# A hybrid decoder step on one Trainium2 core: keys' rotation partners copied by ScalarE, sigmoids made of Tanh

## The reference, cut to what matters

```python
def partial_rope(x, pos):                       # ROT_DIM = 32 of 128 features, half = 16
    x1, x2 = xf[..., :half], xf[..., half:ROT_DIM]
    out = concatenate([x1 * cos - x2 * sin, x2 * cos + x1 * sin, xf[..., ROT_DIM:]])

aq = partial_rope(rms_norm(aq, q_norm_w), pos)
ak = partial_rope(rms_norm(ak, k_norm_w), pos)

def merge_branches(...):
    h = h * sigmoid(mo)
    h = rms_norm(h, mh_norm_w)
    y_att = (attn * silu(az)) @ w_proj_attn
    y_ml = (h * silu(mz)) @ w_proj_mlstm
    return x + (sigmoid(ga) * y_att + sigmoid(gm) * y_ml) @ w_out
```

## Time and profile before

| what | us |
|---|---|
| median of 3 runs | 475.58 |
| lowest, highest | 474.67, 478.96 |
| the profiled execution | 473.98 |
| its span, first to last instruction | 471.9 |
| TensorE (PE) busy | 459.9 |
| VectorE (DVE) busy | 403.4 |
| ScalarE (ACT) busy | 289.8 |
| GpSimd (POOL) busy | 102.7 |

### The profile page before, as it was taken

How to read it: one execution, slowest core, us unless ns; L and a number is a source line. 1 busy time by engine, 2 the same in 40 slices (tenths; PEclk the granted TensorE clock), 3 DMA queues, 4 the chain that set the end, 5 groups by cost and what they waited for, 6 DMA issues and landing times.

```text
span 471.9 us, 11257 instructions
## 1 busy us (share of the span) xinstructions
PE 459.9 (97%) x3823; PEld 417.8 (89%) x3823; DVE 403.4 (85%) x1646; ACT 289.8 (61%) x486; POOL 102.7 (22%) x181
## 2 busy tenths in 40 slices
PE   7999999999989999999999999999999999999997
PEld 5899899898779899888899879889899898899997
DVE  3898899699999997999999999879999964567861
ACT  4866545676973575895575595658857468334430
POOL 2032321013323322513331242322223110000000
PEclk9999999999999999999999999999999999999999
DMA  8697589747799999999999999999999997456511
GB/s 319 237 386 296 194 316 346 247 179 269 271 417 411 413 394 312 329 405 415 412 397 348 393 411 382 412 398 319 350 413 409 417 413 269 167 181 240 182 75 46
DMA packets 36929, 150.89 MB, mean 320 GB/s; under 512 B 5436, under 2 KB 7036, under 8 KB 29576
## 3 DMA queue, kind: packets, MB, share of 16 engines
q1 hardware_dynamic: 12304, 70.77, 39.4%
q0 software_dynamic: 19008, 67.20, 37.1%
q10 hardware_dynamic: 5560, 12.21, 6.7%
HBM read 137.37 MB, written 12.76 MB: 318 GB/s over the span
## 4 chain that ended last, share of the span: by engine, by line
PE 69%; DVE 13%; ACT 9%; DMA 4%; issue 4%; ACTq 0%; POOL 0%; SPq 0%; DVEq 0%; POOLq 0%
PE pj L533 25%; PE pj L536 12%; PE wk L533 8%; PE pa L714 4%; PE wk L536 4%; DVE w L1070 4%; DVE kpages L1169 3%; DMA cslot<-in_states 2%; ACT w L816 2%; DVE cslot L1253 2%; ACT L836 2%; DMA out_C_s<-cslot 2%; PE wk L486 2%; PE wk L638 1%; PE wk L670 1%
## 5 line engine op out<-in xcount | busy, mean ns | idle before, releaser
L533 PE MATMUL pj<-xn,w 128*128 128x264 f32 x1328 | 180.6, 288 | 0.8 <-ACT mqT L974 0.7
L533 PEld LDWEIGHTS pj<-xn,w 128*128 128x128 f32 x1328 | 168.4, 189 | 8.8 <-issue 6.6
L1070 DVE TENSOR_TENSOR w<-wraw,w 128x1024 fp32r<-128x1024 f32 x112 | 136.1, 1219 | 10.1 <-ACT w L816 9.6
L816 ACT ACTIVATE w<-wraw 128x1024 fp32r<-128x1024 f32 x112 | 117.9, 1053 | 31.6 <-PE wk L536 13.0
L1169 DVE CUSTOM_DVE_ANT_0 kpages<-kpages,qbc 128x128 f32<-128x128 f32 x512 | 114.7, 286 | 0.6 <-DMA kpages<-in_cache_k 0.4
L536 PE MATMUL pj<-xn,w 128*128 128x264 f32 x664 | 94.4, 284 | 3.6 <-DVE w L1070 3.6
L536 PEld LDWEIGHTS pj<-xn,w 128*128 128x128 f32 x664 | 85.5, 188 | 4.7 <-DVE w L1070 4.7
L403 POOL DMA_DIRECT2D kpages<-in_cache_k x64 | 34.3, 536 | 175.5 <-DVE sco L1169 151.8
L403 POOL DMA_DIRECT2D vpages<-in_cache_v x64 | 33.9, 530 | 65.0 <-issue 39.3
L1169 DVE DVE_READ_ACCUMULATOR2_ANT sco<- 128x1 f32 x512 | 40.9, 80 | 0.0
L714 PE MATMUL pa<-vpages,prob 128*32 128x256 f32 x512 | 34.3, 385 | 0.8 <-ACT prob L874 0.8
(11 more groups left out here) (277 smaller groups left out, 640.8 us busy)
## 6 DMA issues: line engine op xcount, KB each, us to landing
wraw<-in_weights SPq DMA_DIRECT2D x56, 1024.0 KB, 7.9
kpages<-in_cache_k POOLq DMA_DIRECT2D x64, 512.0 KB, 8.2
vpages<-in_cache_v POOLq DMA_DIRECT2D x64, 512.0 KB, 10.5
cslot<-in_states SPq DMA_DIRECT2D x16, 512.0 KB, 10.9
out_C_s<-cslot ACTq DMA_DIRECT2D x16, 512.0 KB, 8.0
xres<-in_tokens SPq DMA_DIRECT2D x1, 1056.0 KB, 7.8
out_k_p<-kT ACTq DMA_DIRECT2D x4, 256.0 KB, 11.9
out_v_p<-v_nat ACTq DMA_DIRECT2D x4, 256.0 KB, 6.4
```

The costliest lines, as they stand in the source:

```text
L533: mm(bank[:, 0:T], w2[:, q, 0, k, :], src[:, g, k, :], start=(k == 0 and g == 0), stop=False)
L816: A(w2[:, n % WSPLIT, 0], wraw[:, pair % WRAW, :, (n % 2) * P:(n % 2 + 1) * P], ACT.Copy).then_inc(whi_ready, 1)
L1070: V.tensor_tensor(w2[:, q, 1], wraw[:, slot, :, half * P:(half + 1) * P], w2[:, q, 0], ALU.subtract).then_inc(wlo_ready, 1)
```

## The change

Three things. (1) The features of queries and keys are put in another order by the host, so that a rotated feature's partner stands 32 partitions away (features 0 to 15 in partitions 0 to 15, features 16 to 31 in partitions 32 to 47); constants, norm weights and outputs follow. For the keys, ScalarE copies partitions 32 to 63 of the raw head to partitions 0 to 31 of a new tile `swapped`, and 0 to 31 to 32 to 63; the sign is in the sine table. VectorE reads `swapped` on 64 partitions, and the rotation matmul of the keys is gone, with two waits of TensorE. Queries keep their rotation on TensorE. The decode queries' rows are made by a product with a permutation matrix in place of a transpose. (2) Each sigmoid becomes a Tanh of half the argument; the half and the plus one go into evictions, weights and the products on VectorE. (3) The chain of small gate operations on VectorE, spread over heads 1 to 3, runs at head 0.

```diff
 query_rows (TensorE)
-                    last = tr(bank[0:NB, ...], qT[:, h, SEQ:T], P)
+                    last = mm(bank[0:NB, ...], qT[:, h, SEQ:T], back, start=True, stop=True)
 keys_side (TensorE)
                         pe.wait_ge(c_ready, NB * j - 2) if j else pe.wait_ge(q_ready, HEADS)
-                        pe.wait_ge(attg_ready, 2 * j)
                     else:
                         pe.wait_ge(c_ready, NB * j) if j else pe.wait_ge(qs_ready, 2)
-                        pe.wait_ge(mrs_ready, j + 1)
-                    norm_sums(wk[2 * n], wk[2 * n + 1], n, kT[:, n, :])
+                    mm(wk[2 * n][:, 0:T], ones, sq[:, n, :], start=True, stop=True).then_inc(norm_ps, 1)
 ScalarE
-                A(zsig[:, 1], zraw[:, 1], ACT.Sigmoid).then_inc(sig_ready, 1)
+                A(zsig[:, 1], zraw[:, 1], ACT.Tanh).then_inc(sig_ready, 1)
 (the same at L949, L959 and, with scale=0.5, at L1055; the evictions to zraw get scale 0.5)
-                    A(sq[:, :, :], hT[:, :, :], ACT.Square).then_inc(sqh_ready, 1)
+                    A(sq[:, :, :], hT[:, :, :], ACT.Square, scale=0.5).then_inc(sqh_ready, 1)
                 split_hi(n + AHEAD)
+                if i < 2:
+                    ch.join()
+                    act.wait_ge(kT_ready, 2 * j)
+                    A(swapped[0:LO, i], kT[LO:2 * LO, i, :], ACT.Copy)
+                    A(swapped[LO:2 * LO, i], kT[0:LO, i, :], ACT.Copy).then_inc(swap_ready, 1)
 VectorE
+            ch.step(V.tensor_scalar(mhw, mhw, 0.5, None, ALU.mult))
-            def rope_norm(x, r, ro, done):
-                ch.step(V.tensor_tensor(hT[:, 0, :], ro[:, 0:T], sin, ALU.mult))
-                ch.link(V.tensor_tensor(x, x, cos, ALU.mult))
-                ch.link(V.tensor_tensor(x, x, hT[:, 0, :], ALU.add))
+            def rope_norm(x, r, partners, rows, done):
+                part = slice(0, rows)
+                ch.step(V.tensor_tensor(hT[part, 0, :], partners, sin[part], ALU.mult))
+                ch.link(V.tensor_tensor(x[part], x[part], cos[part], ALU.mult))
+                ch.link(V.tensor_tensor(x[part], x[part], hT[part, 0, :], ALU.add))
                 V.tensor_tensor(x, x, r, ALU.mult).then_inc(done, 1)
-                if h == 1:
+                if h == 0:
                     dve.wait_ge(gate_ln, 1)
...
-                if h == 2:
...
-                if h == 3:
...
-                    dve.wait_ge(norm_ps, HEADS + 2 * j + n + 1)
+                    dve.wait_ge(swap_ready, 2 * j + n + 1)
-                    rope_norm(kT[:, n, :], rs[:, n, :], wk[2 * n + 1], kT_ready)
+                    rope_norm(kT[:, n, :], rs[:, n, :], swapped[:, n, :], 2 * LO, kT_ready)
-                    V.tensor_tensor(zraw[:, 0], zraw[:, 0], zsig[:, 0], ALU.mult).then_inc(silu_ready, 1)
+                    V.scalar_tensor_tensor(out=zraw[:, 0], in0=zsig[:, 0], scalar=1.0, in1=zraw[:, 0], op0=ALU.add, op1=ALU.mult)\
+                        .then_inc(silu_ready, 1)
 (the same form at L1317, L1328, L1418 and L1422; L1432 multiplies by 0.5 as it adds the residual)
```

More of the change, by code:

```diff
@@ L239, in build @@
         rot = cst[:, C_ROT:C_ROT + P]
+        back = cst[:, C_BACK:C_BACK + P]
         mask3 = cst[:, C_MASK:C_MASK + 384]
@@ L561, in query_rows @@
                 for h in range(first, first + 4):
-                    last = tr(bank[0:NB, (h - first) * P:(h - first + 1) * P], qT[:, h, SEQ:T], P)
+                    last = mm(bank[0:NB, (h - first) * P:(h - first + 1) * P], qT[:, h, SEQ:T], back, start=True, stop=True)
                 last.then_inc(qs_ps, 1)
@@ L948, in _ @@
                     act.wait_ge(evac, n)
-                    A(zraw[:, 2], zraw[:, 2], ACT.Sigmoid).then_inc(sig_ready, 1)
+                    A(zraw[:, 2], zraw[:, 2], ACT.Tanh).then_inc(sig_ready, 1)
                     fade_states(j, 1)
@@ L1054, in _ @@
                     act.wait_ge(proj, n + 1)
-                    A((sga, sgm)[m][:, c, :], banks[i % 4][:, 0:T], ACT.Sigmoid).then_inc(sg_ready, 1)
+                    A((sga, sgm)[m][:, c, :], banks[i % 4][:, 0:T], ACT.Tanh, scale=0.5).then_inc(sg_ready, 1)
                 elif m == 3:
@@ L1316, in states_side @@
                     ch.join()
-                    V.tensor_tensor(hT[:, :, :], hT[:, :, :], zraw[:, 2], ALU.mult).then_inc(hmo_ready, 1)
+                    V.scalar_tensor_tensor(out=hT[:, :, :], in0=zraw[:, 2], scalar=1.0, in1=hT[:, :, :], op0=ALU.add, op1=ALU.mult)\
+                        .then_inc(hmo_ready, 1)
                 if i == 15:
@@ L1327, in round_close @@
                 dve.wait_ge(sig_ready, 3 * j + 3)
-                ch.step(V.tensor_tensor(zraw[:, 1], zraw[:, 1], zsig[:, 1], ALU.mult))
+                ch.step(V.scalar_tensor_tensor(out=zraw[:, 1], in0=zsig[:, 1], scalar=1.0, in1=zraw[:, 1], op0=ALU.add, op1=ALU.mult))
                 dve.wait_ge(mrs_ready, j + 2)
@@ L1431, in _ @@
                         dve.wait_ge(xres_load, 16)
-                    V.tensor_tensor(yout[:, c, :], banks[(i - 1) % 4][:, 0:T], xres[:, c, :], ALU.add).then_inc(ep_y, 1)
+                    V.scalar_tensor_tensor(out=yout[:, c, :], in0=banks[(i - 1) % 4][:, 0:T], scalar=0.5, in1=xres[:, c, :],
+                                           op0=ALU.mult, op1=ALU.add).then_inc(ep_y, 1)
 def two_sided(x):
@@ L1448, in constants @@
     for m in range(half):
-        c[m + half, C_ROT + m] = -1.0
-        c[m, C_ROT + m + half] = 1.0
+        c[m + LO, C_ROT + m] = 1.0
+        c[m, C_ROT + m + LO] = 1.0
+    c[np.arange(P), C_BACK + ORDER] = 1.0
     r = np.arange(P)
@@ L1477, in weight_pairs @@
 def weight_pairs(w_in, w_proj_mlstm, w_proj_attn, w_out):
-    cuts = [w_in[:, AQ + 256 * n:AQ + 256 * (n + 1)] for n in range(4)]
-    cuts += [w_in[:, g + 256 * j:g + 256 * (j + 1)] for j in range(JOBS) for g in GROUPS]
+    pair = np.concatenate([ORDER, HD + ORDER])
+    cuts = [w_in[:, AQ + 256 * n + pair] for n in range(4)]
+    cuts += [w_in[:, g + 256 * j + (pair if g == AK else np.arange(256))] for j in range(JOBS) for g in GROUPS]
     for w in (w_in[:, GA:GA + D], w_in[:, GM:GM + D], w_proj_mlstm, w_proj_attn, w_out):
@@ L1505 @@
         "consts": constants(),
-        "columns": np.concatenate([cols(n) for n in ("norm_w", "q_norm_w", "k_norm_w", "mh_norm_w")], axis=1),
+        "columns": np.concatenate([cols("norm_w"), cols("q_norm_w")[ORDER], cols("k_norm_w")[ORDER], cols("mh_norm_w")], axis=1),
         "tokens": np.concatenate([np.ascontiguousarray(inputs["x_prompt"])[0], np.ascontiguousarray(inputs["x_sample"])[:, 0]]).T
@@ L1523 @@
     y = g["y"].reshape(P, KC, T).transpose(2, 1, 0).reshape(T, D)
-    k_p = g["k_p"].transpose(3, 0, 2, 1).reshape(rows)
+    there = np.argsort(ORDER)
+    k_p = g["k_p"][:, there].transpose(3, 0, 2, 1).reshape(rows)
     v_p = g["v_p"].reshape(JOBS, P, 2, 256).transpose(2, 1, 0, 3).reshape(rows)
@@ L1531 @@
     return (y[:SEQ].reshape(1, SEQ, D), y[SEQ:].reshape(NB, 1, D), k_p, v_p, C_p, n_p, g["m_p"].reshape(1, 1, MH),
-            by_sample(g["k_s"]), by_sample(g["v_s"]), C_s, n_s, g["m_s"])
+            by_sample(g["k_s"][there]), by_sample(g["v_s"]), C_s, n_s, g["m_s"])
```

26 lines of the change are left out of this document (16 added, 10 removed).

## The result

The kernel after takes 477.85 us (median of 20 runs, 475.02 to 479.43) against 475.08 us before (20 runs, 473.41 to 478.96): ratio 1.0058, 95% interval 1.0042 to 1.0074. That is 2.8 us slower, inside the forecast's range and inside "within 1%", but 1.7 us more than the sum of +1.1. The forecast's range is 10.5 us wide, so that it holds the time says little of the sum. The profiled execution took 478.32 us (span 476.2), against 473.98 of before.

A forecast was written before the change was run, and what follows sets the result against it. TensorE was taken to bound the kernel, except two stretches around the starts of jobs 1 and 2 where VectorE does. Terms -0.90 + 0.72 + 0 + 0 + 1.32 gave +1.1 us, forecast 475.9 us, range 469.5 to 480.0.

The forecast's parts named there:

- The case: The forecast itself, 50%: TensorE-bound kernel with two VectorE-bound stretches, copies lengthening ScalarE's unbroken work in job 3; +1.1 us.
- TensorE bounds throughout: Rival, 22%: removed rotation products count in full and both waits for ScalarE go; -4.4 us.
- Tanh in another set: Rival, 10%: Tanh loads from another set than Exp, so table loads stay and jobs 1 to 3 pay for copies; +2.2 us.
- Job 0, -0.90 + 0.72: Where TensorE bounds, two key rotation products removed save 0.90 us; products for the decode query rows add 0.72 us.
- Job 1, 0: At its start VectorE bounds, so removed rotations gain nothing; 1.32 us of copies stand against one saved load of 1.28.
- Job 2, 0: At its start two saved loads, 2.57 us, outweigh 1.32 us of copies on ScalarE, but VectorE bounds; 0.
- Job 3, +1.32: At its start four copies delay ScalarE's page probabilities, for which TensorE waits; +1.32 us, bounds +1.04 and +1.72.
- about 3 us: Sign of being right: TensorE's wait for the page probabilities in job 3 grows from 0.8 us to this.
- copies far from 0.33 us apart: Sign of being wrong: ScalarE's copies not spaced at the 0.33 us each that the forecast assumed.
- The copies delay every later job: Rival, 13%: copies at 0.43 us each delay the starts of jobs 1 to 3, 1.72 us a job; +5.0 us in all.
- Sum: Total of the forecast's terms over the kernel: -0.90 + 0.72 + 0 + 0 + 1.32 = +1.1 us.
- VectorE over 97% busy: Sign of being right: VectorE's busy share in the stretches with the starts of jobs 1 and 2.

The follow-up runs named there:

- e1: Kernel after with the keys' rotation back on TensorE and without the 16 copies: 474.36 us, 0.9991 of before.
- e3: Kernel after with the keys' rotation back on TensorE and the 16 copies still made into a tile nothing reads: 477.55 us, 1.0056 of before.
- e8: Kernel after with only the second key head's two copies moved from step 1 to the end of step 2: 476.01 us, 1.0022 of before.
- e4: Kernel after with the table set holding Ln and Exp loaded once behind each output gate's Tanh: 475.93 us, 1.0013 of before.
- e6: Kernel before with only Tanh for sigmoid and the common Ln and Exp set loaded once behind the output gate's: 474.65 us, 1.0004 of before.
- e2: Kernel after with Sigmoid and the plain products back, copies kept: 478.46 us, 1.0067 of before.
- e7: Kernel after with the exchanged halves copied straight from PSUM between the key's eviction and its square: 477.57 us, 1.0059 of before.
- e9: Kernel after with the common Ln and Exp set loaded once and the keys only normed, not rotated: 473.00 us, 0.9963 of before.
- e12: Kernel after with the common set loaded once, two triangle additions behind step 0's page scores, gate chain back at heads 1 to 3: 473.78 us, 0.9989 of before.

## Why the prediction was right, and where it was off

**The case** was the right one: TensorE's instructions go where it waits anyway, and copies in ScalarE's unbroken stretch of job 3 set the time (e1, e3). "TensorE bounds throughout" fell: the waits for ScalarE grew instead of going. "Tanh in another set" fell: exactly 14 loads went.

**Job 0, -0.90 + 0.72**: -0.18 foreseen, -0.20 in the trace (+0.76 in the query rows, where the forecast had 0.72, and -0.89 with the two rotations). **Job 1, 0**: right. The trace has -0.20 up to step 9 (TensorE gains the rotation's 0.44 by step 2 and waits it away by step 4) and +0.09 at the end of the job. The +0.29 came late in the job, after VectorE had stood 2.58 us for a page of keys at 159.60, which it does in this execution and not in that of before; neither the loads nor the copies stand there.

**Job 2, 0: this step failed.** It put two loads (2.57 us) against 1.32 us of copies and left the rest to VectorE. But the load at the page probabilities stands in front of an eviction that waits for TensorE. ScalarE in step 0 of job 2, before and then after:

```profile
192.13 1.28 ACT L874 ACT_TABLE_LOAD   x1
193.42 0.26 ACT L874 ACTIVATE prob<-prob 128x64 f32<-128x64 f32 x1
193.68 0.48 ACT L831 ACTIVATE kT<-pj,cols 128x264 f32<-128x264 f32 x1
```

```profile
192.52 0.26 ACT L877 ACTIVATE prob<-prob 128x64 f32<-128x64 f32 x1 [0.32 <-DVE prob L1212]
193.77 0.48 ACT L834 ACTIVATE kT<-pj,cols 128x264 f32<-128x264 f32 x1 [0.99 <-PE pj L540]
```

The eviction comes no earlier, so that load is worth nothing, and one load (1.28) stands against 2.05 us of copies: the mqT eviction comes at 207.63 instead of 206.91. TensorE, rid of its product and so there sooner, waits 2.08 us for it. At full clock VectorE hides such a wait, as the step said: in e8 it is 1.0 us and in e3 1.62, and TensorE leaves the place with no loss against before in either (-0.16 us ahead of it and -0.32 behind it in e8, +0.62 and +0.49 in e3). What it couldn't hide is that the clock fell behind the wait, and the 16 products took 3.44 us instead of 2.23.

**Job 3, +1.32: mechanism right, size off.** The wait of "about 3 us" is 3.01. But copies far from 0.33 us apart, one of the prediction's signs of being wrong, are there too. The term was 4 x 0.33 us, from overlapping neighbours; measured is 4 x 0.51 = 2.05, above the upper bound of 1.72, because a copy starts only when the one before it has ended (0.43) and each pair also waits for the hi half to end (0.14). On top come 0.86 us for the page values at half clock (1.93 instead of 1.07), and 0.6 us for the projection behind them, of which most is made up by the end.

**The copies delay every later job (13%)** priced them at 0.43 each, nearer to the 0.51 than the forecast's 0.33. In the profiled execution it was right on jobs 2 and 3 and wrong on job 1. **Sum**: -0.20 + 0.29 (late in job 1) + 1.22 (job 2, the clock) + 2.05 + 0.86 = +4.2 at step 4 of job 3, and +4.35 at the end, for the two profiled executions. The medians are only 2.8 apart, mainly because that execution of before is 1.1 us faster than the median of before, and that of after 0.5 slower than its own. A fall of the clock was in no term. That the time came out inside the range all the same is owed to the width of the range.

**VectorE over 97% busy** at the starts of jobs 1 and 2 held (98 and 99% in after), and turned out to reach further than the prediction said: it is second in line in job 3 too (e4, e6), and with it the rows' late landing, and that is why taking 33 us of table loads off ScalarE (e6) moves nothing.

The loads inside the inverse root, of which the prediction left open whether they could go, do go when the kernel asks for the common set (e4). The Trainium skill, "ScalarE: Activation LUTs", Rules for kernel authors, says to use natural_log_exp_and_others where both are needed, one load and not two; the trace agrees, 22 loads became 10.

## What to carry to other kernels

Price an instruction put into an engine's unbroken stretch by the distance between starts of the same shape, and against the eviction that some other engine waits for next; what the engine saves before an idle gap can't be set against it. Here one pair of copies moved behind the next eviction took the loss from 2.8 to 1.0 us in the medians.

If three engines stand within 2 us of one another at a place, freeing the last shows only the next: ScalarE, then VectorE, then a small transfer that lands late. Look at each engine's idle time there before counting a gain.

A wait of TensorE of 2 to 3 us can cost more than its length: here some 1 us more, each time the clock fell.

## What the runs showed of the hardware that was not expected

**The clock fell behind waits.** It fell from 2.4 to 1.2 GHz behind waits of TensorE of 2.08 and 3.01 us (after), 2.16 and 3.02 (e2), 2.56 (e3), 2.13 (e7) and 1.89 (e9); it stayed full behind 1.62 (e3), 1.99 (e8), 2.03 (e4), 2.19 (e6) and 2.34 (e12). Windows of e3 (clock third from the end), whose wait of 1.62 us ended at 208.6 and that of 2.56 at 283.1:

```profile
209.00:213.00 4.00, 4.00 (x35) 4.00 (x35) 3.90 (x21) 3.95 (x6) 1.05 (x2) 1.00 1.01 417
...
284.00:288.00 4.00, 4.00 (x23) 3.86 (x20) 3.90 (x20) 3.95 (x6) 0.45 (x2) 0.57 0.99 365
```

Waits of the same length are on both sides, so the length alone doesn't decide; what else does wasn't tried.

The 20 runs of after fall into four groups by mean clock: 1.000 (3 runs, median 476.0 us), 0.996 (5, 477.0), 0.993 (8, 478.1) and 0.989 (4, 479.2). The profiled execution, with two stretches at half clock, has 0.993, and that of e3, with one, has 0.996. So the groups are, by estimate, runs with none, one, two and three such stretches, and one more costs 1.0 to 1.1 us.

**Copies from 32 partitions to 32 others don't overlap with their neighbours.** They start 0.43 us apart within SBUF and 0.48 us apart from PSUM, each after the end of the one before, while full evictions of 264 columns start 0.38 us apart and two copies of 8 x 256 0.26 us. The copies of 8 partitions stay in the partitions they come from and do overlap, which speaks for the shift and not for the small number; 32 partitions without a shift weren't tried. The Trainium skill, "ScalarE: Activation LUTs", What ACT_TABLE_LOAD costs, has back-to-back ACTIVATEs overlap by about 93 ns; these don't.

**The transfer of a short row took 8.7 to 10.3 us** from issue to landing in job 3 (before and e6, the longest of their four; 1.9 us in job 0 of both), and this spread reaches TensorE through VectorE.
